# Start addresses of the activations: buffers for two layers laid 64 bytes apart, and the rest of the on-chip memory moved by 64 bytes

## What is computed

```python
for l in range(2):
    last = l == 1
    xn  = rmsnorm(h,  norm1_g[l]) * (1 + sc1)  + sh1
    xnc = rmsnorm(hc, norm1_g[l]) * (1 + sc1c) + sh1c
    if last: ckv_c = xnc @ w_in[l][:, OFF_KV:OFF_GATE]      # context: keys and values alone
    else:    proj_c = xnc @ w_in[l]; ckv_c = proj_c[..., OFF_KV:OFF_GATE]
    k_c, v_c = mla_kv(ckv_c, ...)
    h = h + g1 * token_mix(xn @ w_in[l], k_c, v_c, ...)
    h = h + g2 * sq_relu_mlp(rmsnorm(h, norm2_g[l]) * (1 + sc2) + sh2, w_ff1[l], w_ff2[l])
    if not last:
        hc = hc + g1c * token_mix(proj_c, k_c, v_c, ...)
        hc = hc + g2c * sq_relu_mlp(...)
return rmsnorm(h, final_g)

def token_mix(proj, ...):                     # three branches, three gates
    a = pool_mixer(proj[pool]) @ pool_out
    b = hyena_mixer(proj[hy]) @ hy_out        # long convolution by a Fourier transform
    c = attention(proj[q, kv]) @ w_o
    return (ga * a + gb * b + gc * c) @ w_out

def sq_relu_mlp(x, w1, w2):                   # 1024 -> 4096 -> 1024
    return square(relu(x @ w1)) @ w2
```

## Time and profile before

| | us |
|---|---|
| median of 3 runs | 1565.12 |
| lowest, highest | 1561.71, 1566.65 |
| span of the profiled execution | 1561.9 |
| PE busy in it | 1462.9 (94%) |
| DVE, ACT, POOL busy | 917.7, 622.2, 228.9 |

### The profile page before, as it was taken

The page is one execution under the profiler, slowest core; times in us unless marked ns, Lnnn a source line. Parts: engine busy times, 40 slices in busy tenths (PEclk is TensorE's granted clock), DMA queues, the critical chain, the costliest instruction groups (busy, mean ns, idle before and its releaser), DMA issues.

```text
span 1561.9 us, 21399 instructions
## 1 busy us (share of the span) xinstructions
PE 1462.9 (94%) x7698; PEld 1153.6 (74%) x7698; DVE 917.7 (59%) x1214; ACT 622.2 (40%) x896; POOL 228.9 (15%) x203
## 2 busy tenths in 40 slices
PE   3799999999999999799999999997999999899997
PEld 0265766867887776577777777875868898899996
DVE  5875656364554477755544555227776575776664
ACT  4442345154232244544333443113354453454451
POOL 5400100240201133100000000221002301500003
PEclk9899999999999999899999999997999999999999
DMA  6522210355421236345444543222313573546562
GB/s 246 199 89 87 94 54 1 115 181 189 161 94 55 65 122 204 108 162 175 162 148 161 172 160 128 94 92 68 122 68 125 172 244 109 161 150 195 183 189 79
DMA packets 56565, 210.21 MB, mean 135 GB/s; under 512 B 6213, under 2 KB 7365, under 8 KB 55600
## 3 DMA queue, kind: packets, MB, share of 16 engines
q1 hardware_dynamic: 54176, 194.22, 38.2%
q0 software_dynamic: 2320, 15.04, 2.5%
HBM read 205.57 MB, written 3.67 MB: 134 GB/s over the span
## 4 chain that ended last, share of the span: by engine, by line
PE 85%; DVE 8%; ACT 3%; issue 1%; POOL 1%; DMA 1%; SPq 0%; DVEq 0%; ACTq 0%; POOLq 0%
PE ps L1278 24%; PE ps L1279 23%; PE ps L1280 23%; PE ps L1314 4%; DVE wl L854 3%; PE ps L1496 2%; PE ps L1521 2%; PE ps L1588 1%; PE ps L1598 1%; DVE normed L912 1%; ACT wh L594 1%; PE ps L1508 1%; DMA raw<-in_units 1%; DVE rstd L905 1%; DVE xl L921 1%
## 5 line engine op out<-in xcount | busy, mean ns | idle before, releaser
L854 DVE TENSOR_TENSOR wl<-raw,wh 128x1024 fp32r<-128x1024 f32 x368 | 477.8, 1317 | 236.6 <-ACT wh L594 232.7
L594 ACT ACTIVATE wh<-raw 128x1024 fp32r<-128x1024 f32 x368 | 381.1, 1053 | 342.3 <-PE ps L1280 318.1
L1278 PE MATMUL ps<-xh,wh 128*128 128x512 f32 (+2 forms) x1376 | 476.8, 347 | 34.3 <-DVE xl L921 27.6
L1279 PE MATMUL ps<-xl,wh 128*128 128x512 f32 (+2 forms) x1376 | 469.8, 341 | 0.0
L1280 PE MATMUL ps<-xh,wl 128*128 128x512 f32 (+2 forms) x1376 | 469.2, 341 | 0.0
L1278 PEld LDWEIGHTS ps<-xh,wh 128*128 128x128 f32 (+1 forms) x1376 | 263.3, 191 | 79.2 <-issue 30.7
L1279 PEld LDWEIGHTS ps<-xl,wh 128*128 128x128 f32 (+1 forms) x1376 | 264.1, 192 | 29.8 <-issue 1.0
L1280 PEld LDWEIGHTS ps<-xh,wl 128*128 128x128 f32 (+1 forms) x1376 | 263.7, 192 | 30.1
L1278 PE MATMUL ps<-hid_h,wh 128*128 128x512 f32 (+1 forms) x512 | 171.9, 336 | 0.0
L1279 PE MATMUL ps<-hid_l,wh 128*128 128x512 f32 (+1 forms) x512 | 171.7, 335 | 0.0
L1280 PE MATMUL ps<-hid_h,wl 128*128 128x512 f32 (+1 forms) x512 | 171.7, 335 | 0.0
(11 more groups left out here) (206 smaller groups left out, 1573.3 us busy)
## 6 DMA issues: line engine op xcount, KB each, us to landing
raw<-in_units SPq DMA_DIRECT2D x368, 512.0 KB, 3.5
filters<-filt POOLq DMA_DIRECT2D x2, 1280.0 KB, 5.2
filt<-filters POOLq DMA_DIRECT2D x2, 1280.0 KB, 10.3
ftab<-in_fwd POOLq DMA_DIRECT2D x3, 768.0 KB, 4.6
h<-in_x POOLq DMA_DIRECT2D x1, 2048.0 KB, 17.5
counts<-in_counts POOLq DMA_DIRECT2D x2, 1024.0 KB, 5.1
decay<-in_decay POOLq DMA_DIRECT2D x2, 512.0 KB, 10.3
itab<-in_inverse POOLq DMA_DIRECT2D x2, 512.0 KB, 7.1
```

The source lines that it names most:

```text
L594: act.activation(wh[:, slot, :], raw[:, slot, :], ACT.Copy).then_inc(hi_ready, 1)
L854: dve.tensor_tensor(wl[:, slot, :], raw[:, slot, :], wh[:, slot, :].bitcast(F), ALU.subtract).then_inc(lo_ready, 1)
L1278: pe.matmul(dst, w_h, m_h, start=first, stop=False)
L1279: pe.matmul(dst, w_h, m_l, start=False, stop=False)
```

## The change

Two things are done. First, `by_layer` gives a buffer 128 bytes more room and two views of it, one for each layer, at different starts: `SHIFT` is 16 numbers, or 64 bytes. `xh`, `xl`, `fh`, `fl`, `hid_h`, `hid_l` are now lists, and every use takes the view of its layer (`v // 2` is the layer of a norm). Second, a new buffer `pad` of 64 bytes stands ahead of the reused room, and three fillers grow by what `fh` and `fl` grew.

```diff
+SHIFT = 16
...
+        def by_layer(scope, name, blocks, shifts):
+
+            room = alloc(scope, name, (blocks * T + 2 * SHIFT,), R)
+            return [room[:, at:at + blocks * T].rearrange("p (k t) -> p k t", t=T) for at in shifts]
...
-        xh = alloc(ctx, "xh", (KB, T), R)
-        xl = alloc(ctx, "xl", (KB, T), R)
+        xh_of = by_layer(ctx, "xh", KB, (0, SHIFT))
+        xl_of = by_layer(ctx, "xl", KB, (0, SHIFT))
...
         KBYTE = 256
+        alloc(ctx, "pad", (16,))
...
-            fh = alloc(s, "fh", (4, T), R)
-            fl = alloc(s, "fl", (4, T), R)
+            fh_of = by_layer(s, "fh", 4, (0, SHIFT))
+            fl_of = by_layer(s, "fl", 4, (SHIFT // 2, SHIFT + SHIFT // 2))
...
-            alloc(s, "pad_d", (16 * KBYTE,))
+            alloc(s, "pad_d", (16 * KBYTE + 4 * SHIFT,))
...
-            alloc(s, "pad_f", (4 * KBYTE,))
+            alloc(s, "pad_f", (4 * KBYTE + 4 * SHIFT,))
...
-            hid_h = alloc(s, "hid_h", (16, T), R)
-            hid_l = alloc(s, "hid_l", (16, T), R)
+            hid_h_of = by_layer(s, "hid_h", 16, (0, SHIFT))
+            hid_l_of = by_layer(s, "hid_l", 16, (0, SHIFT))
...
-                    blocks(ps[:, bank, 0:n], (p.g0 + j) % SLOTS, xh, xl, n, turn=turns(p, it, j)).then_inc(unit_done, 1)
+                    blocks(ps[:, bank, 0:n], (p.g0 + j) % SLOTS, xh_of[layer], xl_of[layer], n, turn=turns(p, it, j)).then_inc(unit_done, 1)
```

More of the change, by code:

```diff
@@ L621, in norm_hi @@
                     t = slice(s * SEQ, (s + 1) * SEQ)
-                    last = act.activation(xh[:, m, t], normed[:, m, t], ACT.Identity, bias=mods[:, shift, m, s:s + 1])
+                    last = act.activation(xh_of[v // 2][:, m, t], normed[:, m, t], ACT.Identity, bias=mods[:, shift, m, s:s + 1])
                 last.then_inc(x_hi, 1)
@@ L773, in _ @@
                         wait_result(act, p, j, g)
-                        act.activation(fh[:, g, 0:n], ps[:, 2 + (p.dve0 + g) % 2, 0:n], ACT.Copy, scale=pool_scale[:, layer, g:g + 1])\
+                        act.activation(fh_of[layer][:, g, 0:n], ps[:, 2 + (p.dve0 + g) % 2, 0:n], ACT.Copy, scale=pool_scale[:, layer, g:g + 1])\
                            .then_inc(pool_hi[layer], 1)
@@ L818, in hidden_hi @@
                         act.wait_ge(relu2_ready, it * p.mains + (r0 + i + 3))
-                        act.activation(hid_h[:, it * p.mains + i, 0:n], relu2[:, i % 2, 0:n], ACT.Copy).then_inc(hid_hi, 1)
+                        act.activation(hid_h_of[layer][:, it * p.mains + i, 0:n], relu2[:, i % 2, 0:n], ACT.Copy).then_inc(hid_hi, 1)
                     def body(it, p=p, r0=r0, n=n):
@@ L1260, in hidden_lo @@
                         dve.wait_ge(hid_hi, it * p.mains + (r0 + i + 1))
-                        dve.tensor_tensor(hid_l[:, it * p.mains + i, 0:n], relu2[:, i % 2, 0:n],
-                                          hid_h[:, it * p.mains + i, 0:n].bitcast(F), ALU.subtract).then_inc(hid_ready, 1)
+                        dve.tensor_tensor(hid_l_of[layer][:, it * p.mains + i, 0:n], relu2[:, i % 2, 0:n],
+                                          hid_h_of[layer][:, it * p.mains + i, 0:n].bitcast(F), ALU.subtract).then_inc(hid_ready, 1)
                     if layer == 0 and half == "a":
@@ L1293, in blocks @@
                         pe.wait_ge(mod_copied, 2 * turn + 2)
-                    if mh is mixh:
+                    if any(mh is v for v in mixh_of):
                         moving = mh[:, 0:n // SEQ, k, :], ml[:, 0:n // SEQ, k, :]
@@ L1543, in branch_out @@
                 def branch_out(name, ready, before):
-                    mh, ml = (mixh, mixl) if name == "hy_out" else (fh, fl)
+                    mh, ml = (mixh_of[layer], mixl_of[layer]) if name == "hy_out" else (fh_of[layer], fl_of[layer])
                     for j, p, slot in straight(layer, name):
@@ L1553, in _ @@
                     bank = act_bank(p, 0, j, 0)
-                    blocks(ps[:, bank, 0:n], slot, xh, xl, n).then_inc(unit_done, 1)
+                    blocks(ps[:, bank, 0:n], slot, xh_of[layer], xl_of[layer], n).then_inc(unit_done, 1)
                 gates(layer, "a0")
@@ L1567, in hy_main @@
                     bank = dve_bank(p, it, i, p.mains)
-                    blocks(ps[:, bank, 0:n], (p.g0 + j) % SLOTS, xh, xl, n).then_inc(unit_done, 1)
+                    blocks(ps[:, bank, 0:n], (p.g0 + j) % SLOTS, xh_of[layer], xl_of[layer], n).then_inc(unit_done, 1)
                 loop(layer, "hy", hy_main)
@@ L1630, in down @@
                             bank = 2 + (p.dve0 + i // 2) % 2
-                        blocks(ps[:, bank, 0:n], (p.g0 + j) % SLOTS, hid_h, hid_l, n, k0=8 * (i % 2),
+                        blocks(ps[:, bank, 0:n], (p.g0 + j) % SLOTS, hid_h_of[layer], hid_l_of[layer], n, k0=8 * (i % 2),
                                first=i % 2 == 0, last=i % 2 == 1, ready=(hid_ready, before) if i < 2 else None,
```

31 lines of the change are left out of this document (16 added, 15 removed).

## The result

The changed kernel takes 1573.28 us, the median of five runs (1571.36 to 1576.95), against 1565.12 us before: a ratio of 1.0049 with a 95% interval of 1.0034 to 1.0064. It is slower by 8 us, where 14 us less was forecast. The profiled execution has a span of 1569.6 us, 7.7 more than before.

The account below looks back on a forecast made before the run. PE's matmul spacing was taken as the bound, set by the moving operand's start address. First layer 7.3 plus second layer net 6.9 gives 14.2 us off the 1565.1 median: 1551 us (chance 0.45), range 1544 to 1564.

Parts of the forecast that it names:

- What bounds the kernel, and that addresses move it: Whole kernel: PE, busy 94% of the span, bounds it; the moving operand's start address sets the spacing of its matmuls.
- The rule "at 0 or at 64 modulo 128": All PE phases: a moving operand starting at 0 is 6.5 ns better for wide matmuls, at 64 for narrow ones.
- The slower rival: First-layer wide `xh`/`xl` matmuls: place against the weights over more than 128 bytes counts, costing 13 us; about 1575 us, chance 0.08.
- First layer, 7.3 us gained: Wide matmuls moved from 64 to 0: ff2 5.0, wo/pool_out/hy_out 1.9, uq/ukv/pool_w 0.7 us, together 7.6, taken as 7.3.
- `fl` as `fh`: wo, pool_out, hy_out: `fl` at 32 and 96 goes with `fh`; first-layer bound 1.9 us gained or none, second layer nothing.
- Second layer, 8.1 us for `xh`/`xl`: Narrow matmuls moved from 0 to 64: ff1a/ff1b 4.9, hy and w_out 1.1, the gates and q 2.1 us.
- the worse rhythm: Rival, second-layer MLP: ff1a locks at 117.7 ns and carries ff2a, ff1b, ff2b with it, losing 6.5 us; 1557.5 us, chance 0.22.
- pool, gate_a0, gate_a1 at nothing: Second layer: up to 1.2 us saved on PE, none at the end, as PE waits longer behind DVE's weight splits.
- kv and kpe, 0.5 us lost, cq 0.2: Second-layer losses: kv and kpe wide at 64, 72 matmuls, 0.5 us; cq narrow at 0, 54 matmuls, 0.2 us.
- DVE and ACT at nothing: Other buffers' moves from 64 to 0 cost DVE and ACT nothing; DVE takes 426 ns for 256 columns either way.
- The Trainium skill's spacing: Opposing rule for PE: spacing by columns alone, N/2.4 + 2.5 ns, 215.7 ns for 512; start addresses would gain zero.

Follow-up runs that it names:

- the version with 32 bytes: Changed kernel with rooms 256 bytes larger, second-layer shift 192 bytes, and `fl` 32 bytes further on in both layers, timed against the kernel before: 1550.5 us (0.9918).
- the version with both halves at 192: Changed kernel with rooms 256 bytes larger, `fl` at `fh`'s start, and a second-layer shift of 192 bytes for all six buffers: 1551.8 us (0.9920), repeated 1552.0.

## Why the prediction was wrong, point by point

**What bounds the kernel, and that addresses move it:** right. Addresses alone made medians from 1550.5 to 1573.3 us, with the same instructions and nearly the same waits.

**The rule "at 0 or at 64 modulo 128": wrong, and this is the step that failed.** Its rows were right and showed two distances from the weights, 0 and 192 modulo 256; I read them as two starts. No row could tell the two readings apart, since `wh` and `wl` stood at one place in all of them. The slower rival named the right quantity, and I gave it 0.08 because of `uh`. But `uh` differs from `hid` by 256 bytes, and the change moved `xl` by 128. That row excluded the one distance that does nothing (moving the weights by 256 shows it) and said nothing of the other. The starts modulo 512 in the section on the change had it all: 128 and 256 beside 384. That rival's 1575 us lies near the 1573.3 measured, but not by its terms: it had 13 us lost by `xh`/`xl` in the first layer and 4 won in the second, where 9.2 and another 0.4 were lost.

**First layer, 7.3 us gained:** 1.5 us, of `hid` 1.0 and `fh`/`fl` 0.5, since their low halves had parted as well, and `xh`/`xl`, for which the sum had nothing, lost 9.2. With the distances kept, the two large terms come out as worked out: `hid` -4.8 (5.0 forecast), `fh`/`fl` -1.9 (1.9), so the sizes were right and the condition was not. uq, ukv and pool_w gave 0.3 of their 0.7 in every version.

**`fl` as `fh`:** wrong, and inside the bounds given. In the change, 160 bytes apart modulo 256, and in the version with 32 bytes it costs 1.3 to 1.4 of the 1.9 us.

**Second layer, 8.1 us for `xh`/`xl`:** 3.6, and `hid` lost 3.4. The numbers are those of the worse rhythm, 45.2 us for both ff1b and ff2b, but it is not shown that this is the rival as I described it. The halves had parted here too, to 64 and 192, and no narrow phase of `xh`/`xl` or `hid` ran at 113.3 ns in the change, nor in the run that undid `xl`'s part, where `hid` still lay so; the distances alone may have excluded it. Where both halves lie at 192 the two rhythms do differ between executions of one program, by 5.9 us where I had 6.5. There the forecast's fault is that it gave the kernel one rhythm or the other.

**pool, gate_a0, gate_a1 at nothing:** nearly. DVE, then PE, in the changed kernel:

```profile
1226.00 0.43 DVE L1154 TENSOR_TENSOR ul<-padded,uh 128x256 fp32r<-128x256 f32 x1 [1.89 <-ACT uh L613]
...
1226.95 3.66 DVE L862 TENSOR_TENSOR wl<-raw,wh 128x1024 fp32r<-128x1024 f32 x3 [0.52 <-ACT wh L602]
...
1231.15 0.55 PE L1286 MATMUL ps<-uh,wh 128*128 128x256 f32 x1 [3.82 <-DVE fl L1159]
```

PE's wait grows from 3.51 us to 3.82, the same three splits take the same 3.66, and the 0.4 us that PE saves in the three phases is given back. A wait of 4 us or more was forecast for a larger saving, and that is what the version with both halves at 192 shows, where the three phases save 1.3 us:

```profile
1219.98 0.55 PE L1286 MATMUL ps<-uh,wh 128*128 128x256 f32 x1 [4.84 <-DVE fl L1159]
```

**kv and kpe, 0.5 us lost, cq 0.2:** 0.2 (16.46 to 16.64 us) and 0.0.

**DVE and ACT at nothing:** right, 919.0 and 622.6 us against 917.7 and 622.2.

**The Trainium skill's spacing:** the runs disagree with what the prediction took from it. The page "TensorE: Matmul & The Clock Gate" (Back-to-back issue gap) has N/2.4 + 2.5 ns, some 216 ns for 512 columns, but calls that the gap of an isolated matmul, and gives about 131 ns for a sustained stream of weight loads and matmuls of 512 columns. The runs here, which are such streams in float32, have neither: 226.7 to 233.3 ns at 512 columns and 113.3 to 120.0 at 256, by where four buffers lie. The page's step-by-step section says that loading the next weights takes no read bandwidth from the running matmul. Moving `wl` alone changes the spacing (231.1 ns instead of 226.8), so either that does not hold for every pair of addresses, or something else in PE depends on the two together. The runs don't tell which.

## What to carry to other kernels

Where PE is the bound and its operands are float32, work out for each matmul how the moving operand starts against its weights modulo 256 bytes, for high and low halves each. With 512 float32 columns put all four at one remainder; with 256 columns 64 bytes off it (192 was better here than 64: 1551.8 and 1552.0 us against 1558.8). Give every filler or double-view room a size that is a multiple of 256 bytes, or it moves all that stands behind it. And before a rule read off addresses is built on, move everything together by the step in question: if the phases stay, the rule is not about the start itself.

## What the runs showed of the hardware

- The spacing of float32 matmuls depends on the distance between moving operand and weights modulo 256 bytes, by up to 2.9% at 512 columns (226.7 to 233.3 ns) and 5.9% at 256 (113.3 to 120.0). Moving every buffer by 64 bytes, or the weights by 256, or `raw` by 128, changes none of the four phases read.
- At one and the same layout PE can settle in one of several rhythms (113.3 or 117.8 ns with 256 columns at a distance of 192), which holds for hundreds of matmuls and over a change of operand, and differed between two executions of one program. In the four executions compared it is there within five matmuls of the rise of the granted clock.
- Open: what gives parted halves three rhythms, whether 64 and 192 together ever give 113.3, why 64 and 192 differ for wide matmuls but both give 113.3 or 117.8 for narrow ones, and how the rise of the clock could be timed so as to get 113.3. Distances other than 0, 32, 64, 96, 128 and 192 were not tried.
